# Moving the recurrence and the preparation of the forgetting attention behind the input projection, and both attentions into one pipeline

## The reference, cut to what matters

```python
proj = jnp.einsum('bsd,de->bse', h, w_in)
q_a, k_a, v_a, x_b, g_b, q_c, k_c, v_c, f_c = jnp.split(proj, IN_SPLITS, axis=-1)
y_a = sliding_window_sink_attention(q_a, k_a, v_a, sinks)      # 8 query heads, 2 key heads, window 128
x_conv = causal_depthwise_conv(x_b, conv_w, conv_b)
y_b = rg_lru(x_conv, ...) * jax.nn.gelu(g_b)                   # a_t * h + u_t over the tokens
log_f = jax.nn.log_sigmoid(f_c + fox_bf)                       # 4 heads
y_c = forgetting_attention(q_c, k_c, v_c, log_f)               # logits + cum_q - cum_k, causal
y = concatenate([rms_normalize(y_a), rms_normalize(y_b), rms_normalize(y_c)])
```

## Time and profile before

| what | value |
|---|---|
| median of the runs before | 3729.96 us (three: 3725.9, 3729.96, 3734.28) |
| time of the profiled execution | 3728.16 us |
| its span, first to last instruction | 3726.4 us |
| TensorE busy | 3093.0 us (83%) |
| VectorE busy | 1753.2 us (47%) |
| ScalarE busy | 1202.6 us (32%) |
| GpSimd busy | 446.5 us (12%) |
| mean granted TensorE clock | 0.906 |

### The profile page before, as it was taken

The page is one execution under the profiler, slowest core; times in us unless marked ns, Lnnn a source line. Parts: engine busy times, 40 slices in busy tenths (PEclk is TensorE's granted clock), DMA queues, the critical chain, the costliest instruction groups (busy, mean ns, idle before and its releaser), DMA issues. The chain is left out here.

```text
span 3726.4 us, 40110 instructions
## 1 busy us (share of the span) xinstructions
PE 3093.0 (83%) x16033; PEld 2448.5 (66%) x16033; DVE 1753.2 (47%) x2668; ACT 1202.6 (32%) x1837; POOL 446.5 (12%) x411
## 2 busy tenths in 40 slices
PE   5679869899987999997997789979999684565985
PEld 3467536688875888886775457758787463345774
DVE  3664455323246555535316533355554434243886
ACT  3212445311114211212325442233222332223774
POOL 2240113100010000001402220010000010201111
PEclk8789989999998999999899899989999786785997
DMA  4773010222112443421610113316553220014993
GB/s 153 152 149 112 8 21 1 52 60 60 51 40 74 124 118 104 120 80 39 96 53 1 21 44 92 85 52 182 168 180 91 43 59 1 13 45 149 347 330 119
DMA packets 422057, 343.42 MB, mean 92 GB/s; under 512 B 34338, under 2 KB 369264, under 8 KB 421744
## 3 DMA queue, kind: packets, MB, share of 16 engines
q1 hardware_dynamic: 407088, 296.14, 27.6%
q0 software_dynamic: 14784, 44.71, 4.9%
HBM read 335.49 MB, written 24.15 MB: 97 GB/s over the span
## 5 line engine op out<-in xcount | busy, mean ns | idle before, releaser
L902 PE MATMUL ps<-ahi,w_hi 128*128 128x512 f32 (+1 forms) x2384 | 868.9, 364 | 172.6 <-DVE alo L655 84.4
L903 PE MATMUL ps<-ahi,w_lo 128*128 128x512 f32 (+1 forms) x2384 | 856.5, 359 | 0.0
L904 PE MATMUL ps<-alo,w_hi 128*128 128x512 f32 (+1 forms) x2384 | 856.4, 359 | 0.0
L902 PEld LDWEIGHTS ps<-ahi,w_hi 128*128 128x128 f32 x2384 | 460.9, 193 | 260.4 <-issue 60.0
L924 DVE TENSOR_TENSOR w_lo<-w_raw,w_hi 128x1024 fp32r<-128x1024 f32 (+2 forms) x248 | 357.7, 1444 | 426.4 <-ACT w_hi L914 425.5
L904 PEld LDWEIGHTS ps<-alo,w_hi 128*128 128x128 f32 x2384 | 460.3, 193 | 68.0
L903 PEld LDWEIGHTS ps<-ahi,w_lo 128*128 128x128 f32 x2384 | 462.3, 194 | 63.7
L914 ACT CAST w_hi<-w_raw 128x1024 fp32r<-128x1024 f32 (+2 forms) x248 | 289.9, 1171 | 478.8 <-PE ps L904 348.3
L736 DVE SCALAR_TENSOR_TENSOR vec_acc<-vec_w,csilu,vec_acc 128x512 f32<-128x512 f32 x364 | 264.0, 771 | 29.3 <-DMA vec_w<-in_w_mod 25.1
L1368 POOL TENSOR_SCALAR prob<-prob,nm 128x512 f32<-128x512 f32 (+4 forms) x104 | 164.3, 1580 | 678.3 <-DVE nm L1293 678.3
L902 PE MATMUL ps<-hhi,w_hi 128*128 128x512 f32 (+1 forms) x528 | 189.3, 359 | 10.1 <-DVE hlo L1033 10.1
(11 more groups left out here) (396 smaller groups left out, 5016.1 us busy)
## 6 DMA issues: line engine op xcount, KB each, us to landing
vec_w<-in_w_mod SPq DMA_DIRECT2D x128, 512.0 KB, 4.2
w_raw<-in_w_in SPq DMA_DIRECT2D x104, 512.0 KB, 4.3
e_raw<-in_w_gate SPq DMA_DIRECT2D x46, 512.0 KB
e_raw<-in_w_up SPq DMA_DIRECT2D x46, 512.0 KB
e_raw<-in_w_down SPq DMA_DIRECT2D x46, 512.0 KB
w_raw<-in_w_ffn_gate SPq DMA_DIRECT2D x44, 512.0 KB, 3.9
w_raw<-in_w_ffn_up SPq DMA_DIRECT2D x44, 512.0 KB, 3.8
w_raw<-in_w_ffn_down SPq DMA_DIRECT2D x32, 704.0 KB, 4.7
```

Of the source, the lines that this page charges most:

```text
L902: pe.matmul(o, whi[:, j, b0 + b, :], hi[:, b, t0:t0 + tn], start=(b == 0), stop=False)
L903: pe.matmul(o, wlo[:, j, b0 + b, :], hi[:, b, t0:t0 + tn], start=False, stop=False)
L904: m = pe.matmul(o, whi[:, j, b0 + b, :], lo[:, b, t0:t0 + tn], start=False, stop=(b == nb - 1))
```

## The change

A class `Branches` is given to `run_dense` as `background`, and its GpSimd program as `pool_program`. The order of the pieces becomes recurrence input (2), gate (2), keys and values of the banded attention, keys (2) and values (2) of the forgetting attention, its queries (2), and the queries of the banded attention (4). Step by piece number:

- SyncE: loads of the forget weights, their bias and the mask (0); the 16 small transfers of the gate weights, after a wait for their zeroed tile (1); bias table and sinks, with a wait for both (4).
- TensorE: the forget rows as 24 products with four stationary columns (2), 4 small transposes (3), 4 gate products (4), 4 small transposes (5), 4 small transposes and 4 products that spread the cumulated rows to all partitions (6), 12 transposes of the values (12).
- VectorE: convolution (1, 2), one softplus of 18 columns (3), the cumulated sum as a scan over 4 rows (5), `a0*a0` and `(1 + a0^2) * tanh` in place of the reciprocal and its two neighbours (6), the rest of the recurrence (9 to 11).
- ScalarE: the rounding (0), the bias (2), Exp (3), sigmoids (4), Exp and Tanh (5), copies of `ck` (6), Sqrt (8), Tanh of the gelu (9), copies of the values (12).
- GpSimd: keys, the first three steps of the gelu, the 32 steps of the decay tables, and the negation of the bias table.

The result of the recurrence stays in `xc` and goes to `normalize` as `src`. The 16 and the 8 units then form one list for one `Heads` pipeline. The triangle is no longer loaded, and the 96 tiny products, the 20 products of L2049 and the 16 of L2055 are gone. The softplus itself (some 24 dependent steps) is unchanged.

```diff
+        class Branches:
+            ORDER = (S_XB, S_XB + 1, S_GB, S_GB + 1, S_KA, S_VA, S_KC, S_KC + 1, S_VC, S_VC + 1, S_QC, S_QC + 1, 0, 1, 2, 3)
+            BANKS = (1, 2, 3, 5)
...
+            def copied(self, eng, tile_):
+                n = self.ORDER.index(tile_)
+                eng.wait_ge(psum_free[n % 2].sem, self.c0[psum_free[n % 2]] + n // 2 + 1)
...
+            def sp(self, sp, n):
+                if n == 0:
+                    sp.dma_start(self.fw[:], g["w_in_2"][0][:, 16 * P:16 * P + FOX_H].rearrange("(k p) c -> p k c", p=P)).then_inc(fox_w_in.sem, 16)
+                    sp.dma_start(self.bf[:, 0:1], g["fox_bf_2"][0].rearrange("(h a) -> h a", a=1)).then_inc(fox_w_in.sem, 16)
+                    sp.dma_start(self.causal[:], g["k_causal"]).then_inc(causal_in.sem, 16)
+                if n == 1:
+                    sp.wait_ge(wbd_zero.sem, 1)
+                    for s, name in enumerate(("lru_wa_2", "lru_wx_2")):
+                        for b in range(8):
+                            q = 32 * (b % 4)
+                            sp.dma_start(self.wbd[q:q + 32, s, b // 4, q:q + 32], g[name][0, b]).then_inc(lru_w_in.sem, 16)
+                if n == 4:
+                    sp.dma_start(self.bt[:], g["k_swa"]).then_inc(swa_in.sem, 16)
+                    sp.dma_start(self.sinks[:], g["sinks_2"][0].partition_broadcast(P)).then_inc(swa_in.sem, 16)
+                    sp.wait_ge(swa_in.sem, 32)
...
+            def pe(self, pe, n):
+                if n == 2:
+                    pe.wait_ge(fw_lo.sem, 1)
+                    for k in range(KT):
+                        o = ps[0:FOX_H, 6 * BANK:6 * BANK + LAT]
+                        pe.matmul(o, self.fw_hi[:, k, :], self.ahi[:, k, :], start=(k == 0), stop=False)
+                        pe.matmul(o, self.fw_hi[:, k, :], self.alo[:, k, :], start=False, stop=False)
+                        m = pe.matmul(o, self.fw_lo[:, k, :], self.ahi[:, k, :], start=False, stop=(k == KT - 1))
+                    m.then_inc(f_rows.sem, 1)
+                if n == 3:
+                    pe.wait_ge(f_neg.sem, 1)
                     for t in range(4):
+                        m = pe.transpose(ps[:, 7 * BANK + 4 * t:7 * BANK + 4 * t + 4], self.fT[:, t * P:(t + 1) * P], ident[0:FOX_H, 0:FOX_H])
+                    m.then_inc(f_cols.sem, 1)
+                if n == 4:
+                    pe.wait_ge(lru_w_in.sem, 256)
+                    pe.wait_ge(conv_done.sem, 2)
+                    for s in range(2):
+                        for k in range(2):
+                            pe.matmul(self.bank(2 * s + k), self.wbd[:, s, k, :], self.xc[:, k, :], start=True, stop=True).then_inc(gates_mm.sem, 1)
+                if n == 5:
+                    pe.wait_ge(soft_out.sem, 1)
+                    for t in range(4):
+                        m = pe.transpose(ps[0:FOX_H, 6 * BANK + t * P:6 * BANK + (t + 1) * P], self.soft[:, 4 * t:4 * t + 4], ident[:])
+                    m.then_inc(soft_rows.sem, 1)
+                if n == 6:
+                    pe.wait_ge(cum_done.sem, 1)
+                    for t in range(4):
+                        m = pe.transpose(ps[:, 7 * BANK + 4 * t:7 * BANK + 4 * t + 4], self.cum[:, t * P:(t + 1) * P], ident[0:FOX_H, 0:FOX_H])
+                    m.then_inc(cq_mm.sem, 1)
+                    pe.wait_ge(gates_act.sem, 4)
+                    for h in range(FOX_H):
+                        pe.matmul(self.bank(h), self.sel[:, h, :], self.cum[:], start=True, stop=True).then_inc(ck_mm.sem, 1)
+                if n == 12:
+                    self.copied(pe, S_VC + 1)
+                    self.copied(pe, S_VC)
+                    pe.wait_ge(ck_copied.sem, FOX_H)
+                    for t in range(4):
+                        for q, v in enumerate((S_VA, S_VC, S_VC + 1)):
+                            o = BANK * self.BANKS[t] + q * P
+                            m = pe.transpose(ps[:, o:o + P], self.proj[:, v, t * P:(t + 1) * P], ident[:])
+                        m.then_inc(v_turned.sem, 1)
...
+            def act(self, act, n):
+                if n == 0:
+                    act.wait_ge(fox_w_in.sem, 32)
+                    act.copy(self.fw_hi[:], self.fw[:]).then_inc(fw_hi.sem, 1)
+                if n == 2:
+                    act.wait_ge(f_rows.sem, 1)
+                    act.wait_ge(soft_ready.sem, 1)
+                    act.activation(self.fT[:], ps[0:FOX_H, 6 * BANK:6 * BANK + LAT], ACT.Identity, scale=-1.0, bias=self.bf[:, 1:2]).then_inc(f_neg.sem, 1)
+                if n == 3:
+                    act.wait_ge(soft_in.sem, 1)
+                    act.activation(self.e[:], self.e[:], ACT.Exp).then_inc(soft_exp.sem, 1)
+                if n == 4:
+                    for q in range(4):
+                        dst, b = ((self.r, V3_BA), (self.ig, V3_BX))[q // 2]
+                        act.wait_ge(gates_mm.sem, q + 1)
+                        act.activation(dst[:, q % 2, :], self.bank(q), ACT.Sigmoid, bias=col(vec3, b + q % 2)).then_inc(gates_act.sem, 1)
+                if n == 5:
+                    act.wait_ge(soft_out.sem, 2)
+                    act.wait_ge(gates_act.sem, 4)
+                    for k in range(2):
+                        act.activation(self.a0[:, k, :], self.r[:, k, :], ACT.Exp, scale=self.sc[:, k:k + 1]).then_inc(a_exp.sem, 1)
+                    for k in range(2):
+                        act.activation(self.tmp[:, k, :], self.r[:, k, :], ACT.Tanh, scale=self.sc[:, 2 + k:3 + k]).then_inc(a_exp.sem, 1)
...
+                    dve.wait_ge(soft_rows.sem, 1)
+                    dve.tensor_tensor_scan(self.cum[:], ones[0:FOX_H, 0:1].to_broadcast([FOX_H, LAT]), ps[0:FOX_H, 6 * BANK:6 * BANK + LAT], 0.0,
+                                           ALU.mult, ALU.add).then_inc(cum_done.sem, 1)
+                    dve.wait_ge(gates_act.sem, 4)
+                    dve.wait_ge(conv_done.sem, 2)
+                    ch.link(dve.tensor_tensor(self.ig[:], self.ig[:], self.xc[:], ALU.mult))
+                if n == 6:
+                    dve.wait_ge(cq_mm.sem, 1)
+                    dve.tensor_copy(self.cq[:], ps[:, 7 * BANK:7 * BANK + 16].rearrange("p (t h) -> p t h", h=FOX_H)).then_inc(cq_copied.sem, 1)
+                    dve.wait_ge(a_exp.sem, 4)
+                    ch.link(dve.tensor_tensor(self.sq, self.a0[:], self.a0[:], ALU.mult))
+                    dve.scalar_tensor_tensor(out=self.tmp[:], in0=self.sq, scalar=1.0, in1=self.tmp[:], op0=ALU.add, op1=ALU.mult).then_inc(u_square.sem, 1)
...
+            def pool(self, pool):
+                gb = self.proj[:, S_GB:S_GB + 2, 0:LAT]
+                self.copied(pool, S_KA)
+                for kv in range(2):
+                    for j in range(2):
+                        pool.tensor_copy(self.kd[64 * j:64 * j + HD, kv, :], self.proj[64 * kv:64 * kv + HD, S_KA, 0:LAT]).then_inc(pool_chain.sem, 1)
+                p0 = pool_chain.base + 4
+                pool.wait_ge(pool_chain.sem, p0)
+                for k in range(2):
+                    self.copied(pool, S_GB + k)
+                pool.wait_ge(a_exp.sem, 4)
+                pool.tensor_tensor(self.r[:], gb, gb, ALU.mult).then_inc(pool_chain.sem, 1)
+                pool.wait_ge(pool_chain.sem, p0 + 1)
+                pool.tensor_scalar(self.r[:], self.r[:], 0.044715, 1.0, ALU.mult, ALU.add).then_inc(pool_chain.sem, 1)
+                pool.wait_ge(pool_chain.sem, p0 + 2)
+                pool.tensor_tensor(self.r[:], self.r[:], gb, ALU.mult).then_inc(gelu_in.sem, 1)
+                pool.wait_ge(causal_in.sem, 16)
+                pool.wait_ge(cq_copied.sem, 1)
+                p = p0 + 2
+                for h in range(FOX_H):
+                    pool.wait_ge(ck_copied.sem, h + 1)
+                    for t in range(4):
+                        pool.tensor_scalar(self.decay[t][:, h, :], self.ck[:, h, 0:(t + 1) * P], -1.0, self.cq[:, t, h:h + 1], ALU.mult, ALU.add).then_inc(pool_chain.sem, 1)
+                        p += 1
+                        pool.wait_ge(pool_chain.sem, p)
+                        d = self.decay[t][:, h, t * P:(t + 1) * P]
+                        pool.tensor_tensor(d, d, self.causal[:], ALU.subtract)
+                pool.wait_ge(swa_in.sem, 32)
+                pool.tensor_scalar(self.bt[:], self.bt[:], -1.0, None, ALU.mult)
...
+                attend(Heads(c, units))
...
-                    banded_attention(proj)
-                    recurrence(proj)
-                    forgetting_attention(proj, ahi, alo)
+                            branches.prepare(c2, xn[:])
+                            run_dense(new_ring(c2, KT), norm=norm, background=(branches,), pool_program=branches.pool,
+                                      layers=[project(g["w_in_2"][0], proj, first, n, LAT, first * P, (ahi, alo), scale)
+                                              for first, n, scale in ((S_XB, 4, None), (S_KA, 2, None), (S_KC, 4, None), (S_QC, 2, -NA_SCALE), (S_QA, 4, -NA_SCALE))])
```

(37 more changed lines are left out.)

343 lines of the change are left out of this document (104 added, 239 removed).

## The result

| what | before | after |
|---|---|---|
| median of the runs (us) | 3730.2 (3725.9 to 3734.3) | 3633.4 (3611.1 to 3640.8) |
| ratio, 95% interval | | 0.9731 (0.9687 to 0.9774) |
| profiled execution: its time, span | 3728.2, 3726.4 | 3633.7, 3631.6 |

The kernel became 97 us faster; 120 were forecast, and 3633 us lies above the range of 3598 to 3624. The profiled execution is 24.9 us above the sum made for it (3608.8).

A forecast was written before the change was run, and what follows sets the result against it. TensorE's products bound the projection, chains between engines the stretches behind it. 136.9 us leave, less 15.5 added on TensorE, 1 and 1, gives 119.4; from 3728.16 that makes 3608.8, median 3610 us; range 3598 to 3624.

The forecast's parts named there:

- What leaves: Between the projection's last sum and the last forgetting output: of 202.6 us, 65.7 stay and 136.9 leave.
- The way in: From the projection's last sum to the first maximum: last copy, change of blocks, first scores; 1.4 us, before 7.4.
- the 24 units: Banded and forgetting units in one pipeline: 40.2 us banded plus 24.1 us forgetting.
- The background on TensorE: Work added to TensorE within the projection, paid in full: 15.5 us, bounds 14 and 27.
- the forget rows: 24 products streaming 512 columns through four stationary columns in the projection: 5.5 us, at most 10.
- the gate products: Eight records on TensorE inside the projection at the high clock: 3.4 us, before 6.18.
- the 12 transposes of the values: TensorE transposes added in the projection, 0.13 us each: 1.6 us.
- the 1 us: Added in the projection for VectorE splits held up by GpSimd steps through shared SBUF access: 1 us.
- I take the sum of late weights as it was, 8.3 us, so nothing is added: Late weight loads in the projection cost the same as before; bounds -8.3 and +12 us.
- that rival, at 0.17: Late weights grow: two queued loads land slowly and TensorE's clock falls; up to +12 and 2 us, 3618 to 3625; chance 0.17.
- for TensorE's own waits (...) a whole piece of 5.49 us lies between cause and wait: In the projection TensorE should not wait on `f_neg`, `soft_out` or `cum_done`, a piece of 5.49 us lying between.
- The rival on the clock: TensorE's clock falls under products on four stationary columns, +5 to +7 us, f32 products at most +7; 3615 to 3623; chance 0.10.

The follow-up runs named there:

- e_gates_late: Changed kernel with the sixteen gate-weight loads issued at piece 3 instead of piece 1; 3623.4 us (one run).
- e_bias_late: Changed kernel with bias table and sinks loaded at piece 8 instead of piece 4, without the wait; 3613.4 us, ratio 0.9680 to the kernel before.
- e_scan_early: Changed kernel with VectorE's running sum of the forget rows at piece 4 instead of piece 5, ahead of the late split; 3617.3 us (one run).
- a_again: Changed kernel measured again without an edit, beside the kernel before on one chip; 3627.8 us, ratio 0.9714.
- a_third: Changed kernel measured a third time without an edit; 3624.4 us, ratio 0.9704 to the kernel before.
- e_gap_128: e_late_spread plus an unused tile of 128 bytes a partition ahead of the weight tiles; 3611.3 us (one run).
- e_gap_192: e_late_spread plus an unused tile of 192 bytes a partition ahead of the weight tiles; 3608.3 us, ratio 0.9664 to the kernel before.
- e_late_spread: Changed kernel with bias table at piece 8, no wait, and the four ck products one each behind pieces 6 to 9; 3605.1 us, ratio 0.9669.

## Why the prediction was wrong

**What leaves** held in its sum. The way in was 1.4 us (3081.83 to 3083.23), and the 24 units 64.5, against 64.3. That the latter fits to 0.2 is luck: the banded units up to the first forgetting maximum (3120.38) took 37.2 us instead of 40.2, the rest 27.3 instead of 24.1, two errors of 3 us that cancel; and other executions gave 61.7 to 67.0 in all.

**The background on TensorE** was sized well: of the 24.1 us that the stretch grew by, 3.9 are more idle time (9.06 and 0.54 us, against 2.82 and 2.92 before), 3.7 the `fox_cum` products at the lower clock (7.10 us from start to start, less 3.4), 1.5 piece 6 behind them (7.06 less 5.60), and 1.6 the longer step (15 times 0.11); 1.4 go off, since before a piece too had been slow behind a stop (6.91 less 5.49). That leaves 14.8 for all added work, against 15.5 + 2. Its largest terms came out close: the forget rows 5.55 us against 5.5, the gate products 3.04 against 3.4, the 12 transposes of the values 1.23 against 1.6. VectorE and GpSimd did meet: a split took twice its 1.23 us beside the negation,

```profile
3048.55 2.44 DVE L932 TENSOR_TENSOR w_lo<-w_raw,w_hi 128x1024 fp32r<-128x1024 f32 x1 [3.27 <-ACT w_hi L922]
...
3046.27 5.37 POOL L2028 TENSOR_SCALAR swa_bias<-swa_bias 128x2048 f32<-128x2048 f32 x1
```

and no stop of TensorE came from it, so the 1 us was not needed. The rule quoted from the Trainium skill (SBUF — State Buffer, "Who interferes with whom") agrees with this trace in that the split was held up; it ended at 3050.99, though, 0.65 us ahead of the GpSimd step, so these rows don't show them apart for the whole instruction. The prediction also misread: the slow `a2lo` did not end with the GpSimd step (2940.20) but 0.54 us behind it (2940.74), as if most of its 0.69 us had been done only then.

**The step that failed** is "I take the sum of late weights as it was, 8.3 us, so nothing is added". The lateness grew: that rival, at 0.17, is what happened, though not by the two loads queued at piece 1 that it named (e_gates_late). I had seen that the table and a wait for it stand ahead of piece 6's load, and let the longer pieces pay for it. The queue stood from 2986.8 to 3000.6, 13.8 us, longer than such a piece. Idle time and lower clock together cost 7.7 us more than before (3.9 + 3.7 + 1.5 - 1.4); e_bias_late, with the table behind piece 9's load and no wait, has none of the stop at piece 6 and a stretch of 102.6 instead of 114.7. My upper bound for it (+12 and 2) held. The stretch's miss of 6.5 is this and the longer step, less what the added work came out cheaper. The longer step, 1.6 us here, had no term in the sum at all; it goes with the place of the weight tiles.

**A second step failed with it:** "for TensorE's own waits (...) a whole piece of 5.49 us lies between cause and wait". It lies there only if VectorE is free to do the cause. `cum_done` stood behind a split that waited for a load, and e_scan_early took 5.5 us off by exchanging the two. The rival on the clock had the forget rows first, and these (24 products on 4 columns) ran at 1.00; of the f32 products, which it named as well, it was those on 4 rows under which the clock fell, for about 2 us in e_bias_late.

**What put the time outside the range is not the change's.** Profile against profile, 15.5 of 24.9 us lie ahead of the first load, and the kernel before shows 14.1 there. The other 9.5 us alone would have made some 3619 us of the forecast 3610, inside the range. By the ratios of a_again and a_third, 3730.2 us would become 3623.5 and 3619.8. Counted from the first load to the end, the two profiles of the kernel before have 812.0 and 809.8 us and the three of the changed one 702.1, 702.6 and 701.2: by these five profiles the change is worth about 109 us, not 97 (the three ratios give 100, 107 and 110). Against 119.4 that leaves about 10: 6.5 of the stretch and 2.5 behind the units (1.2 of it the longer step of the output projection: 192 products by 6.5 ns; the rest is open). A range taken from one profiled execution had to hold how far executions differ ahead of the change, and mine held only the median's 1.8 us.

**What the change could give.** With the table loaded at piece 8, the ratio is 0.9680 (3613 us); with the spread products too 0.9669 (3605 us), which is the forecast's size. The first beats the changed kernel on the same chip with the intervals apart (0.9701 to 0.9727). Between the two, and with the moved tiles (0.9664), no difference can be told.

## What to carry to other kernels

A wait in a transfer queue is paid by the load behind it. Ask when that load is wanted, not how long the wait is by itself, and put large loads that are needed late behind those needed soon, with the wait at the consumer. When short background steps go between pieces, put each ahead of anything that can be late on the same engine: the engine that waits for the background will otherwise wait for a load, under another name. And compare a forecast made from one profiled execution with several of the unchanged kernel, since what lies ahead of the change may differ by more than the forecast of the change is off (15.5 us here, against 9.5).

## What was not expected of the hardware

- The place of the tiles in SBUF set the step of a product: 233.3, 228.9 and 226.8 ns for the same instructions, with `w_hi` and `w_lo` at 160, 32 and 96 modulo 256 bytes (the moving tile at 96 each time), as the output projections of after, e_gap_128 and e_gap_192 show. By which mechanism is open; only the three places were seen.
- The granted clock fell to the lower level with TensorE busy throughout, under eight records (3.67 us) of f32 products that fill 4 of 128 rows (e_bias_late, e_scan_early). With two records at a time (1.1 us) between full pieces it stayed at 1.00 (e_late_spread). Forget rows, 128 rows by 4 columns, 5.55 us long, left it at 1.00 (the changed kernel, 2973.0 to 2978.4).
- Two stops of the same length ended differently in one execution of the kernel before: behind 2.82 us of idle time the clock was at 0.50 for 2.7 us, behind 2.92 us at 1.00. Behind the stops of 8.4 to 9.3 us it was always low at first.
- The same 24 units took 61.0 to 66.3 us from one execution to the next, and their clock went with it: 0.89, 0.87 or 0.82. Which of the two is the cause is not shown.
